# Strassen-Winograd products for the gate and up slabs of a two-layer decoder trunk, with two of four weight sums on GpSimd

## What is computed

```python
def swiglu(x, w_gu, w_down):
    g, u = jnp.split(x @ w_gu, 2, axis=-1)
    return (jax.nn.silu(g) * u) @ w_down
# x: (512, 1024), w_gu: (1024, 2 * 2816), w_down: (2816, 1024); four such blocks in all
```

## Time and profile before

| | |
|---|---|
| median of 3 runs | 2398.78 us (2398.60 to 2399.22) |
| span of the profiled execution | 2396.8 us |
| PE busy | 2383.4 us, 99% |
| DVE, ACT, POOL busy | 1057.2, 758.1, 16.8 us |
| DMA | 246.58 MB, mean 103 GB/s |

### The profile page before, as it was taken

How to read it: one execution, slowest core, us unless ns; L and a number is a source line. 1 busy time by engine, 2 the same in 40 slices (tenths; PEclk the granted TensorE clock), 3 DMA queues, 4 the chain that set the end, 5 groups by cost and what they waited for, 6 DMA issues and landing times.

```text
span 2396.8 us, 27107 instructions
## 1 busy us (share of the span) xinstructions
PE 2383.4 (99%) x11536; PEld 2004.0 (84%) x11536; DVE 1057.2 (44%) x1590; ACT 758.1 (32%) x1137; POOL 16.8 (1%) x16
## 2 busy tenths in 40 slices
PE   8999999999999999999999999999999999999998
PEld 8888888888888888888888888888888888888887
DVE  4333246554554643332543332465455647333324
ACT  4222123434442332222232221243344433322211
POOL 0000200000000000000000000000000000000000
PEclk9999999999999999999999999999999999999999
DMA  5332434323223332233232332343223323232232
GB/s 168 105 98 95 145 103 125 93 78 98 88 92 123 115 105 97 88 106 106 88 106 91 103 104 90 103 132 94 87 93 97 104 91 136 93 99 95 90 118 74
DMA packets 210536, 246.58 MB, mean 103 GB/s; under 512 B 10576, under 2 KB 172400, under 8 KB 210416
## 3 DMA queue, kind: packets, MB, share of 16 engines
q1 hardware_dynamic: 209872, 244.33, 31.2%
q10 hardware_dynamic: 544, 0.52, 0.1%
HBM read 238.51 MB, written 6.31 MB: 102 GB/s over the span
## 4 chain that ended last, share of the span: by engine, by line
PE 99%; DVE 0%; DMA 0%; DVEq 0%; ACT 0%; issue 0%
PE main L1340 22%; PE main L1342 22%; PE main L1341 22%; PE main L1440 5%; PE main L1442 5%; PE main L1441 5%; PE side L1441 4%; PE side L1440 4%; PE side L1442 4%; PE main L1423 1%; PE main L1424 1%; PE main L1425 1%; PE side L1360 1%; PE side L1586 0%; PE main L1565 0%; PE side L1542 0%
## 5 line engine op out<-in xcount | busy, mean ns | idle before, releaser
L851 DVE TENSOR_TENSOR wl<-raw,wh 128x1024 fp32r<-128x1024 f32 (+2 forms) x437 | 494.3, 1174 | 794.4 <-ACT wh L574 794.1
L1340 PE MATMUL main<-xh,wh 128*128 128x512 f32 x2128 | 833.2, 392 | 0.0
L1342 PE MATMUL main<-xl,wh 128*128 128x512 f32 x2128 | 829.2, 390 | 0.0
L1341 PE MATMUL main<-xh,wl 128*128 128x512 f32 x2128 | 829.0, 390 | 0.0
L574 ACT ACTIVATE wh<-raw 128x1024 fp32r<-128x1024 f32 (+2 forms) x437 | 420.8, 1014 | 674.8 <-PE main L1342 290.4
L1342 PEld LDWEIGHTS main<-xl,wh 128*128 128x128 f32 x2128 | 399.6, 188 | 83.2
L1340 PEld LDWEIGHTS main<-xh,wh 128*128 128x128 f32 x2128 | 399.6, 188 | 83.0 <-issue 0.3
L1341 PEld LDWEIGHTS main<-xh,wl 128*128 128x128 f32 x2128 | 399.8, 188 | 81.5
L964 DVE SCALAR_TENSOR_TENSOR hp<-main,sil 128x512 f32<-128x512 f32 x88 | 56.7, 687 | 306.3 <-PE main L1342 297.0
L644 ACT ACTIVATE hh<-hp 128x512 fp32r<-128x512 f32 x88 | 54.1, 633 | 353.5 <-DVE hp L964 353.5
L1440 PE MATMUL main<-wh,hh 128*128 128x512 f32 x352 | 137.7, 391 | 0.0
(11 more groups left out here) (246 smaller groups left out, 2175.4 us busy)
## 6 DMA issues: line engine op xcount, KB each, us to landing
raw<-gu SPq DMA_DIRECT2D x173, 512.0 KB, 4.6
raw<-w_in SPq DMA_DIRECT2D x100, 512.0 KB, 4.7
raw<-down SPq DMA_DIRECT2D x80, 512.0 KB, 4.2
raw<-w_branch SPq DMA_DIRECT2D x24, 512.0 KB, 4.1
raw<-w_out SPq DMA_DIRECT2D x16, 512.0 KB, 4.2
raw<-w_in SPq DMA_DIRECT2D x28, 256.0 KB, 3.4
raw<-down SPq DMA_DIRECT2D x16, 256.0 KB, 3.1
spill<-xt SPq DMA_DIRECT2D x8, 512.0 KB, 6.6
```

The costliest lines, as they stand in the source:

```text
L851: ins = V.tensor_tensor(put(wl[slot]), get(raw[slot]), f32(put(wh[slot])), ALU.subtract)
L1340: T.matmul(out, hi, rh(k), start=k == 0, stop=False)
L1341: T.matmul(out, lo, rh(k), start=False, stop=False)
L1342: ins = T.matmul(out, hi, rl(k), start=False, stop=k == kk - 1)
```

## The change

Slabs 2 to 21 of each SwiGLU block are cut otherwise. One slab is now 128 columns of gate and 128 columns of up over the whole model width (`gate_and_up`), loaded as four blocks of 512 values per partition: up and gate of the first half of the width, up and gate of the second half. Seen as a 2 by 2 block matrix (half of the width by gate or up), it meets the tokens as another 2 by 2 block matrix (first or second 256 tokens by half of the width). Instead of eight block products it makes seven, after Strassen and Winograd (`seven`), each 4 tiles times 3 matmuls of 256 tokens, 84 matmuls in all. For that it needs

- four sums of token blocks, made once per SwiGLU block on DVE (`token_sums`), and their high parts (ACT) and low parts (DVE, `sum_low`);
- four sums of weight blocks per slab: two in one GpSimd subtraction with 2 times 512 elements (`sums_13`), two on DVE (`sum_2`, `sum_4`), and the high and low parts of the sums (`sums_13`, `sums_24` on ACT, `low_13`, `low_24` on DVE) and of three plain blocks (`plain_blocks`, `plain_low`);
- four additions on DVE that put the results together from the products (`us`, `cs`), and two copies out of PSUM on ACT (`p1c`, `p5c`).

The blocks `wh` and `wl` become three each; the plain blocks alternate between two, the sums have one. PE works in banks of `sd` and of `pm` in turn. The hidden values stay in `hp` unsplit, and `hh` and `hl` are made in the last of these slabs and beside the down projection. ACT keeps a float32 copy of the turned tokens (`xr`, in `high`) for the token sums. `seven` waits at its start until the hidden values of chunk n-2 are made, for n = 2 those of the first chunk.

```diff
@@ loads
+            def gate_and_up(g, gu, layer, c):
+                slot = g % 2
+                sp.wait_ge(w_lo.sem, 2 * g - 2)
+                w = tiles(gu, layer)
+                for i, (half_, j) in enumerate(((0, 1), (0, 0), (1, 1), (1, 0))):
+                    sp.dma_start(raw[slot][:, 512 * i:512 * i + 512].rearrange("p (k c) -> p k c", c=P),
+                                 w[:, 4 * half_:4 * half_ + 4, c * P + j * DFF:c * P + j * DFF + P]).then_inc(raw_in[slot][half_].sem, 16)
@@ ACT
             def high(v, t):
...
+                    if v % 3 != 1:
+                        act.activation(xr[t // 2][:, 4 * b:4 * b + 4, P * (t % 2):P * (t % 2) + P],
+                                       sd[:, 2 * (t % 2) + b, :].rearrange("p (c t) -> p c t", c=4),
+                                       ACT.Copy).then_inc(*o.up(xraw_ready))
...
+            def plain_blocks(g):
+                act.wait_ge(slab_done.sem, g - 1)
...
+                act.activation(wh[sum_blocks(g)[1]][:, 0:1536], raw[g % 2][:, 512:2048], ACT.Copy).then_inc(*o.up(w_hi))
+            def sums_13(g, first):
...
+                    act.wait_ge(product.sem, sum_product(g - 1, 2))
+                act.wait_ge(t13_ready.sem, sum_no(g) + 1)
+                act.activation(wh[sum_blocks(g)[0]][:, 0:1024], tw[:, 0:2, :].rearrange("p a c -> p (a c)"),
+                               ACT.Copy).then_inc(*o.up(t13_hi))
+            def sums_24(g, first):
...
+                    act.wait_ge(product.sem, sum_product(g - 1, 4))
+                act.wait_ge(t4_ready.sem, sum_no(g) + 1)
+                act.activation(wh[sum_blocks(g)[0]][:, 1024:2048], tw[:, 2:4, :].rearrange("p a c -> p (a c)"),
+                               ACT.Copy).then_inc(*o.up(w_hi))
             def ffn(layer, f):
...
+                for n in range(2, KF):
...
+                    if n + 1 < KF:
+                        plain_blocks(g + 1)
+                    act.wait_ge(product.sem, sum_product(g, 0))
+                    act.activation(p1c[:, :], bank(0)[:, 0:256], ACT.Copy).then_inc(*o.up(p1_copied))
+                    act.wait_ge(product.sem, sum_product(g, 1))
+                    act.activation(p5c[:, :], bank(1)[:, 256:512], ACT.Copy).then_inc(*o.up(p5_copied))
+                    if n + 1 < KF:
+                        sums_13(g + 1, False)
+                        sums_24(g + 1, False)
...
+                    act.activation(sil[0][:, 256:512], cs[:, 0, :], ACT.Silu).then_inc(*o.up(silu_ready))
+                    act.wait_ge(slab_done.sem, g + 1)
+                    act.activation(sil[0][:, 0:256], bank(0)[:, 0:256], ACT.Silu).then_inc(*o.up(silu_ready))
@@ POOL
+            def sums_13(g):
+                for h in range(2):
+                    pool.wait_ge(raw_in[g % 2][h].sem, arrived[g])
+                if sum_no(g):
+                    pool.wait_ge(t13_lo.sem, sum_no(g))
+                    pool.wait_ge(w_lo.sem, 2 * g)
+                w = raw[g % 2].rearrange("p (b c) -> p b c", b=4)
+                G.tensor_tensor(tw[:, 0:2, :], w[:, 0:1, :].broadcast_to([P, 2, 512]), w[:, 1:3, :],
+                                ALU.subtract).then_inc(*o.up(t13_ready))
@@ DVE
             def ffn(layer, f):
+                token_sums(v)
+                sum_low(v, 0)
+                sum_low(v, 1)
+                plain_low(n0 + 2)
+                sum_2(n0 + 2)
+                sum_low(v, 2)
+                sum_4(n0 + 2)
+                low_13(n0 + 2)
+                sum_low(v, 3)
+                low_24(n0 + 2)
+                dve.wait_ge(slab_done.sem, n0 + 2)
...
+                for n in range(2, KF):
...
+                    if more:
+                        plain_low(g + 1)
+                        sum_2(g + 1)
+                        low_13(g + 1)
+                        sum_4(g + 1)
...
+                    dve.wait_ge(product.sem, sum_product(g, 3))
+                    V.tensor_tensor(us[:, 1, :], bank(2)[:, 256:512], p1c[:, :], ALU.add).then_inc(*o.up(u2_ready))
+                    V.tensor_tensor(us[:, 0, :], bank(2)[:, 0:256], us[:, 1, :], ALU.add).then_inc(*o.up(u3_ready))
+                    V.tensor_tensor(cs[:, 2, :], p5c[:, :], us[:, 0, :], ALU.add).then_inc(*o.up(c22_ready))
+                    dve.wait_ge(product.sem, sum_product(g, 4))
+                    V.tensor_tensor(cs[:, 0:2, :], bank(1).rearrange("p (a t) -> p a t", a=2), us[:, :, :],
+                                    ALU.add).then_inc(*o.up(c21_ready))
+                    if more:
+                        low_24(g + 1)
+                    dve.wait_ge(silu_ready.sem, silu_ready.val(layer, 42 * f + 2 * n))
+                    V.scalar_tensor_tensor(out=hp[:, n, :], in0=cs[:, 1:3, :].rearrange("p a t -> p (a t)"), scalar=0.5,
+                                           in1=sil[0][:, :], op0=ALU.mult, op1=ALU.mult).then_inc(*o.up(hid_f))
@@ PE
+            def seven(layer, f, g, n):
...
+                def multiply(out, block, at_, tokens, fresh=True):
...
+                    for k in range(4):
+                        T.matmul(out, W[:, k, :], th[:, k, :], start=fresh and k == 0, stop=False, skip_group_check=not fresh)
+                        T.matmul(out, L_[:, k, :], th[:, k, :], start=False, stop=False, skip_group_check=not fresh)
+                        ins = T.matmul(out, W[:, k, :], tl[:, k, :], start=False, stop=k == 3, skip_group_check=not fresh)
+                pe.wait_ge(hid_f.sem, hid_f.val(layer, 22 * f + n - 1))
+                pe.wait_ge(w_lo.sem, 2 * g + 1)
+                multiply(bank(0)[:, first], a, 0, a11).then_inc(product.sem, 1)
+                pe.wait_ge(t13_lo.sem, i + 1)
+                multiply(bank(1)[:, second], b, 0, (sums_hi[0], sums_lo[0])).then_inc(product.sem, 1)
+                multiply(bank(2)[:, first], b, 1, (sums_hi[1], sums_lo[1])).then_inc(product.sem, 1)
+                pe.wait_ge(w_lo.sem, 2 * g + 2)
+                multiply(bank(2)[:, second], b, 2, (sums_hi[2], sums_lo[2])).then_inc(product.sem, 1)
+                pe.wait_ge(p5_copied.sem, i + 1)
+                multiply(bank(1)[:, second], a, 1, (sums_hi[3], sums_lo[3]), fresh=False)
+                multiply(bank(1)[:, first], b, 3, a22).then_inc(product.sem, 1)
+                pe.wait_ge(p1_copied.sem, i + 1)
+                multiply(bank(0)[:, first], a, 2, a12, fresh=False).then_inc(slab_done.sem, 1)
```

More of the change, by code:

```diff
@@ L178, in build @@
         sil = [tmp(f"sil{i}", 2 * i, [P, SEQ]) for i in range(2)]
-        hp = [tmp(f"hp{i}", 4 + 2 * i, [P, SEQ]) for i in range(2)]
+        cs = tmp("cs", 4, [P, 3, 256])
         positions_in = tmp("positions_in", 8, [P, SEQ], I32)
@@ L463, in ffn @@
                 wd = tiles(down, layer)
[L464 to L467, removed]
+                for j in range(begun, 2):
+                    gate_up(n0 + j, gu, layer, j, 0)
+                for c in range(2, KF):
+                    gate_and_up(n0 + c, gu, layer, c)
                 j = 0
@@ L632, in ffn @@
             def ffn(layer, f):
                 n0 = layer * S_LAYER + f * (S_FFN + S_MIX)
[L634 to L645, removed]
+                v = 2 * layer + f
@@ new lines, in ffn @@
+                sums_24(n0 + 2, True)
+                act.wait_ge(slab_done.sem, n0 + 1)
+                for m in range(2):
+                    act.activation(sil[m][:, :], pm[m][:, :], ACT.Silu).then_inc(*o.up(silu_ready))
+                for n in range(2, KF):
+                    g = n0 + n
+                    bank = (lambda b: sd[:, b, :]) if g % 2 == 0 else (lambda b: pm[b])
+                    if n + 1 < KF:
[7 more added lines that the diff above has]
+                        sums_24(g + 1, False)
+                    else:
+                        split(g + 1)
+                        act.wait_ge(w_lo.sem, 2 * g + 2)
+                        for c in range(4):
+                            hidden_high(layer, f, c)
+                    act.wait_ge(c21_ready.sem, sum_no(g) + 1)
+                    act.wait_ge(hid_f.sem, hid_f.val(layer, 22 * f + n))
+                    act.activation(sil[0][:, 256:512], cs[:, 0, :], ACT.Silu).then_inc(*o.up(silu_ready))
+                    act.wait_ge(slab_done.sem, g + 1)
+                    act.activation(sil[0][:, 0:256], bank(0)[:, 0:256], ACT.Silu).then_inc(*o.up(silu_ready))
@@ L646, in ffn @@
+                split(n0 + KF + 1)
+                act.wait_ge(hid_f.sem, hid_f.val(layer, 22 * f + KF))
+                for c in range(4, 8):
+                    hidden_high(layer, f, c)
                 if f == 0:
@@ L648, in ffn @@
                 for j in range(1, 10):
+                    for c in range(4 * j + 4, min(4 * j + 8, KF)):
+                        hidden_high(layer, f, c)
                     split(n0 + KF + j + 1)
@@ new lines, in ffn @@
+                token_sums(v)
[9 more added lines that the diff above has]
+                dve.wait_ge(slab_done.sem, n0 + 2)
+                for m in range(2):
```

(13 more changed lines are left out.)

177 lines of the change are left out of this document (163 added, 14 removed).

## The result

The changed kernel takes 2363.11 us (median of 4 runs, 2362.42 to 2363.83) against 2398.69 us, a ratio of 0.9851 with a 95% interval of 0.9837 to 0.9865. The forecast was 2358 us, inside 2346 to 2394. The span went from 2396.8 to 2360.6 us, 36.2 us less.

What follows compares the result with a forecast made beforehand. PE was taken as the bound, matmul count times spacing: 2396.8 - 64.0 (matmuls) + 16.6 (block starts) + 3.4 (clock) + 3.2 (norm's tail) = 2356.0 us, plus 2.0 around the span, 2358 us. Range 2346 to 2394.

Steps and rivals of the forecast that it cites:

- The matmuls: PE in slabs: 84 matmuls of 256 tokens at 0.120 us replace 48 at 0.2267, 64.0 us less over all blocks.
- the third rival: PE in slabs: matmul spacing rises to 0.125 us with the PSUM bank changes, 2392 us; chance 0.05.
- DVE and POOL in the steady slabs: Steady slabs: the two exclude each other, yet their serial work nearly fits PE's 10.08 us period; cost 0.
- The loop: Steady slabs: DVE's 7.7 us plus W, with lock hand-overs, run serially in 10.23 us against PE's 10.08.
- W: Steady slabs: length of POOL's subtraction of twice 512 elements, taken as 2.45 us and added to DVE's sum.
- 5 us of reserve: Steady slabs: weight sums ready 0.65 us ahead at block start give 5.0 us for 19 slabs, covering DVE's slip.
- the second rival: Steady slabs: the DVE and POOL loop becomes the bound, W 3.25, loop 11.03 us, 2410 us in all; chance 0.14.
- The start of a block: First seven-product slab: PE waits 4.1 us for hp behind DVE's preparation, four times, 16.6 us; bounds 3 to 6 each.
- The loads: Weight loads in slabs: pieces of 512 bytes, four DMAs per slab, issued 10 us ahead of need; cost 0.
- The clock: After the four block-start waits: low granted clock costs 0 to 1.7 us each; half taken, 3.4 us.
- The norm's tail: Blocks after a norm: POOL's first subtraction may delay DVE's last token tile, PE 1.8 us; 0 to 5.4, taken 3.2.
- DVE goes ahead of POOL when it is late: Steady slabs, rival: plain_low takes the port before POOL, loop 10.7 us, 27 us in all, 2385 us; chance 0.15.

Runs made afterwards that it cites:

- the run aside: Changed kernel plus, in three blocks, a second GpSimd subtraction of constants into unused memory after each of its first 19: 2456.21 us, ratio 1.0239.
- the first experiment: Changed kernel without PE's wait for the hidden values at each block's first seven-product slab: 2338.45 us, ratio 0.9747 against the kernel before.

## Why the prediction was right

**The matmuls.** 0.120 us was right to the thousandth, also with banks changing every 12 matmuls. So the 64.0 us is the firm part, and the third rival is out.

**DVE and POOL in the steady slabs.** Cost 0 was right, and the two do exclude each other: the run aside shows it apart from any dependence. The loop was put at 10.23 us and is 9.88. W was 2.45 from its start; behind `hp`, whose row it overlaps, POOL keeps DVE out for 2.2 us. The prediction needed its 5 us of reserve for a drift that never came, since 9.88 is under 10.08. But the spare time is only 0.20 us per slab, and the second rival pointed at a real edge: with 2.2 us more of POOL's subtractions in the loop the kernel is slower than before. Where the edge lies (the forecast said W of 3.1) was not tried.

**The start of a block.** The forecast was 4.1 us, four times; it was 4.0 to 4.2, released by `hp` as said. The chain is the forecast's too, here in the second block:

```profile
848.42 1.76 DVE L1124 TENSOR_TENSOR wl<-raw,wh 128x1536 fp32r<-128x1536 f32 x1 [0.66 <-ACT wh L716]
...
855.84 1.28 DVE L1180 SCALAR_TENSOR_TENSOR hp<-main,sil 128x512 f32<-128x512 f32 x2
```

From the start of `plain_low` to the end of the first `hp` it is 8.1 us, where the sum had 8.2. The first experiment shows that the wait bought nothing: the banks were free, and the sums were ready in time. The forecast took this wait as a price of the change and did not ask whether it was needed.

**The loads.** They were put at nothing, and no wait of PE is put down to one.

**The clock.** Half of 6.8 us (four times 1.7) was taken as the cost, and it came to 7.4: the clock fell behind all four waits. Three times it cost nearly the full price, 1.6 us, and in the first block 2.7, above the bound of 1.7. Work brought it back each time, as the rule cited from the Trainium skill ("TensorE: Matmul & The Clock Gate", Part 1: The HAM clock gate) has it; the rows above agree. This is the term that was mis-sized, by 4.0 us of the 5 us by which the forecast missed.

**The norm's tail.** 3.2 us was taken out of 0 to 5.4 without a sum behind it; three places of 1.8 us with an even chance would be 2.7. It happened at two of three, and PE waited 1.3 us each time. That the total comes so near is luck.

**The account of the miss.** Forecast 2358.0, measured 2363.1. The clock makes 4.0 of it, the tail -0.5, the four waits 0; 1.1 is the remainder told above, and 0.5 is that the span is now 2.5 us under the median instead of 2.0.

**The rivals.** That DVE goes ahead of POOL when it is late did not come about: in the first experiment DVE was late and POOL still got in behind `hp`, at 9.88 us per slab. It does come about between two subtractions of POOL.

## What to carry to other kernels

A saving in the count of products must be multiplied out with the measured spacing of the smaller matmul: seven for eight at half the tokens was 7.4% here, not 12.5%, and 28 of its 64 us were lost at the seams. Look first at what the first iteration of a new loop waits for; a wait written for the steady state (the buffer of two iterations ago) can hold the first one behind its whole preparation, and a wait of 4 us cost the clock here as well. GpSimd's elementwise work pays only where DVE is not in operations with two SBUF inputs meanwhile, or where it only writes; on two SBUF inputs, DVE alone did the same in 1.22 us that GpSimd did in 2.4 with DVE shut out.

## What the runs showed of the hardware

- After PE waits of 4.0 to 4.2 us the granted clock was 0.50 for 3.4 to 5.9 us of work, in all four blocks; after waits of 1.7 to 1.9 us in one block of four. Behind equal waits the stretch can be longer in another run (5.4 to 5.7 us instead of 3.4) and hide a gain of 3 us made elsewhere.
- GpSimd's subtraction of 1024 float32 elements with two SBUF inputs took 2.38 us undisturbed, DVE's 1.22. While it runs, a DVE operation with two SBUF inputs stands still (0.68 us of work took 2.89), one with an input in PSUM does not (0.68 each), and a GpSimd memset of the same size (0.95 us) does not disturb DVE. A one-input GpSimd operation of 1.50 us cost DVE 0.36 us.
- When GpSimd had two such operations in a row and DVE one waiting, DVE's went between them: 3.80 and 3.92 us for the second instead of 2.4.
